# Order of VectorE's level loop and a second value block in split parts, in the gated-linear-attention mixer of a two-block network

## The reference, cut to what matters

```python
z = x @ w_in                                   # q, k (512 wide each), v (1024), r (1024), gate ranks
loga = log_sigmoid(glr @ gate_w + gate_b) / GLA_TAU
# per direction: decay between positions t >= s is exp(b[t] - b[s]), b = cumsum(loga)
A = einsum('bhtd,bhtsd,bhsd->bhts', q, dec, k) ; o = A @ v (+ carried state)
o = head_norm(o_fwd + o_bwd, norm_g)
h = (silu(r) * o) @ w_out
x = layer_norm(ALPHA * x + h) ; x = layer_norm(ALPHA * x + ec_moe(x))   # 16 experts, 201 MB of weights
```

## Time and profile before

| | |
|---|---|
| median of 3 runs | 1665.46 us (1664.6 to 1666.51) |
| the profiled execution, its own time | 1665.1 us |
| its span, first to last instruction | 1663.3 us |
| mean granted clock of TensorE | 0.902 of full speed |
| TensorE busy | 1324.9 us, 80% of the span |
| VectorE busy | 661.9 us, 40% |
| ScalarE busy | 451.0 us, 27% |
| DMA | 537.91 MB, 323 GB/s over the span |

### The profile page before, as it was taken

The page is one execution under the profiler, slowest core; times in us unless marked ns, Lnnn a source line. Parts: engine busy times, 40 slices in busy tenths (PEclk is TensorE's granted clock), DMA queues, the critical chain, the costliest instruction groups (busy, mean ns, idle before and its releaser), DMA issues.

```text
span 1663.3 us, 20942 instructions
## 1 busy us (share of the span) xinstructions
PE 1324.9 (80%) x8622; PEld 849.0 (51%) x8622; DVE 661.9 (40%) x1083; ACT 451.0 (27%) x736; POOL 23.4 (1%) x47
## 2 busy tenths in 40 slices
PE   9999665375476899994755646559999999999997
PEld 8786121121121486841211212117888889888886
DVE  5664000000010288620000000005877678887767
ACT  4452000000010266510100000003444455654443
POOL 2000000000000100000000000000000000000000
PEclk9999887697696999997976968889999999999999
DMA  9778999999999974899999999999755763075650
GB/s 363 213 297 335 432 430 429 430 431 428 431 431 428 400 280 158 320 384 430 430 430 430 430 430 430 430 427 393 236 177 202 250 205 127 1 254 176 202 202 25
DMA packets 131432, 537.91 MB, mean 323 GB/s; under 512 B 8244, under 2 KB 71988, under 8 KB 104092
## 3 DMA queue, kind: packets, MB, share of 16 engines
q1 hardware_dynamic: 127056, 530.08, 79.8%
q10 hardware_dynamic: 2380, 2.31, 0.9%
q0 software_dynamic: 1920, 4.43, 0.8%
HBM read 534.17 MB, written 2.62 MB: 323 GB/s over the span
## 4 chain that ended last, share of the span: by engine, by line
PE 52%; DMA 37%; DVE 5%; ACT 2%; SPq 2%; issue 1%; DVEq 0%; ACTq 0%
PE bank L952 12%; DMA ring<-in_moe_w_down 10%; DMA ring<-in_moe_w_up 10%; PE bank L2373 9%; PE bank L2411 7%; DMA arena<-in_moe_w_down 7%; PE bank L1516 5%; PE bank L2377 5%; PE bank L1563 5%; DMA moe_slots<-in_moe_w_up 3%; DMA moe_slots<-in_moe_w_down 3%; DMA gk_w<-in_moe_w_up 2%; DMA xT_pair<-in_moe_w_up 2%; PE bank L590 1%; PE bank L1572 1%
## 5 line engine op out<-in xcount | busy, mean ns | idle before, releaser
L1516 PE MATMUL bank<-ring,arena 128*32 128x512 f32 x960 | 216.5, 719 | 74.7 <-DMA arena<-in_moe_w_up 35.6
L868 DVE TENSOR_TENSOR w_lo<-ring,w_hi 128x1024 fp32r<-128x1024 f32 x151 | 183.1, 1222 | 87.3 <-ACT w_hi L863 86.7
L1563 PE MATMUL bank<-ring,arena 128*32 128x512 f32 x496 | 145.9, 718 | 55.7 <-DMA moe_slots<-in_moe_w_down 23.0
L863 ACT ACTIVATE w_hi<-ring 128x1024 fp32r<-128x1024 f32 x151 | 158.7, 1057 | 83.0 <-PE bank L952 37.8
L2373 PE MATMUL bank<-xT_parts,w_hi 128*128 128x512 f32 x496 | 177.1, 399 | 0.0
L1683 DVE TENSOR_TENSOR arena<-arena,bank 64x512 f32<-64x512 f32 x32 | 22.1, 691 | 385.8 <-ACT arena L1623 385.8
L1516 PE MATMUL bank<-moe_slots,arena 128*32 128x512 f32 x352 | 107.6, 766 | 55.0 <-DMA ring<-in_moe_w_up 32.4
L2377 PE MATMUL bank<-xT_parts,w_lo 128*128 128x256 f32 x496 | 139.0, 280 | 0.0
L1516 PEld LDWEIGHTS bank<-ring,arena 128*32 128x32 f32 x960 | 48.7, 128 | 152.0 <-issue 140.4
L1623 ACT ACTIVATE arena<-bank 64x512 f32<-64x512 f32 x32 | 18.9, 589 | 395.8 <-PE bank L1516 395.8
L1516 PE MATMUL bank<-arena 128*32 128x512 f32 x488 | 105.6, 712 | 24.3 <-DMA ring<-in_moe_w_up 14.6
(11 more groups left out here) (381 smaller groups left out, 2481.1 us busy)
## 6 DMA issues: line engine op xcount, KB each, us to landing
ring<-in_moe_w_up SPq DMA_DIRECT2D x24, 2048.0 KB, 39.0
ring<-in_moe_w_down SPq DMA_DIRECT2D x22, 2048.0 KB, 41.5
ring<-in_moe_w_gate SPq DMA_DIRECT2D x20, 2048.0 KB, 39.4
moe_slots<-in_moe_w_gate SPq DMA_DIRECT2D x18, 2048.0 KB, 37.1
arena<-in_moe_w_up SPq DMA_DIRECT2D x14, 2048.0 KB, 37.2
arena<-in_moe_w_gate SPq DMA_DIRECT2D x12, 2048.0 KB, 39.8
ring<-in_w_gate SPq DMA_DIRECT2D x22, 1024.0 KB, 5.1
ring<-in_w_up SPq DMA_DIRECT2D x22, 1024.0 KB, 5.1
```

The lines of the kernel that those rows point to most:

```text
L863: nc.scalar.activation(dst, raw, ACT.Copy).then_inc(hi_ready, 1)
L868: nc.vector.tensor_tensor(lo, raw, hi.bitcast(F32), ALU.subtract).then_inc(split_ready, 1)
L1516: last = nc.tensor.matmul(ps[B_GU[j % 2]][32 * c:32 * c + 32, :], xin[:, j, k, :], w, start=(k == 0), stop=(k == KD - 1), tile_position=(0 ...
L1563: last = nc.tensor.matmul(ps[B_DN[c]][32 * j:32 * j + 32, :], hT[:, j // 2, at:at + CAP], slot_row(ud[j], f % 2)[:, c * HALF:(c + 1) * HAL ...
```

## The change

Three things change. In VectorE's loop, `args(n+2)` moves ahead of `key_query(n+1)`, and some low parts move ahead of `merge(n)`. The value block 1 is split as a whole, like block 0: its first half is no longer plain, so there are two more chunks (30 for 28), two more `hi` and two more `lo`, and TensorE's `project(2)` and `project(3)` become two chunks each. Chunks from 12 on have new numbers: 12 to 15 are block 1, 16 and 17 the split half of block 2, 18 to 21 block 3 and 22 to 29 the output projection. The three buffers are dealt out anew, and ScalarE's list is changed to suit.

```diff
-        MIX_CHUNKS, GLA_CHUNKS, FFN_CHUNKS = 32, 28, 3 * NF
+        MIX_CHUNKS, GLA_CHUNKS, FFN_CHUNKS = 32, 30, 3 * NF
...
-                    sp.wait_ge(chunk_done, (ml_mix.done(29), gla_mix.done(25))[m])
+                    sp.wait_ge(chunk_done, (ml_mix.done(29), gla_mix.done(27))[m])
...
-        gla_mix = Mixer(gla_u[0:6] + gla_u[7:10:2] + gla_u[10:16], 2, chunk0["gla"],
-                        {c: -c % 3 for c in range(10, GLA_CHUNKS)})
-        HALF_FIRST = (8, 12, 14, 16)
-        WHOLE_SPLIT = (0, 3)
+        gla_mix = Mixer(gla_u[0:8] + gla_u[9:16], 2, chunk0["gla"],
+                        {c: (GLA_CHUNKS - 1 - c) % 3 for c in range(11, GLA_CHUNKS)})
+        HALF_FIRST = (8, 12, 16, 18)
+        WHOLE_SPLIT = (0, 1, 3)
...
-                elif n in (2, 4):
-                    value_rows(n // 2 - 1)
-                    hi(act, 12 + n)
+                elif n == 2:
+                    value_rows(0)
+                    hi(act, 14)
                 elif n == 3:
-                    hi(act, 15)
+                    hi(act, 15, 16)
+                elif n == 4:
+                    hi(act, 17)
+                    value_rows(1)
                 elif n == 5:
-                    hi(act, 17, 18)
+                    hi(act, 18, 19)
                 elif n == 6:
                     near_blocks()
                     block_merge(5)
-                    hi(act, 19)
+                    hi(act, 20, 21)
...
             for n in range(len(LEVELS)):
+                if n + 2 < len(LEVELS):
+                    args(n + 2)
                 if n + 1 < len(LEVELS):
                     key_query(n + 1)
+                lo(dve, *{2: (15,), 3: (17,), 5: (19,), 6: (21,)}.get(n, ()))
                 if n < BLOCK_LEVEL:
                     merge(n)
-                if n + 2 < len(LEVELS):
-                    args(n + 2)
-                if n < 6:
-                    lo(dve, *((12, 13), (14,), (15,), (16,), (17, 18), (19,))[n])
-            lo(dve, 20, 21)
+                lo(dve, *{0: (12, 13), 1: (14,), 2: (16,), 4: (18,), 5: (20,)}.get(n, ()))
+            lo(dve, 22, 23)
```

More of the change, by code:

```diff
@@ L969, in token_chunk @@
                 self.products(pe, c, [(ps[banks[i]][:, :], slice(k2 * HALF, (k2 + 1) * HALF),
-                                       (slice(None), c % 4 * 2 + k2, slice(i * P, (i + 1) * P)),
-                                       not onto and c % 4 * 2 + k2 == 0, c % 4 * 2 + k2 == KD - 1, False)
+                                       (slice(None), (c - self.count) % 4 * 2 + k2, slice(i * P, (i + 1) * P)),
+                                       not onto and (c - self.count) % 4 * 2 + k2 == 0, (c - self.count) % 4 * 2 + k2 == KD - 1,
+                                       False)
                                       for i in tiles for k2 in range(2)], operand, more=tiles == (0,))
@@ L2072, in gla_scalar @@
                     value_rows(3)
-                    hi(act, 20, 21)
+                    hi(act, 22, 23)
             head_std(act, 1, 0)
@@ L2078, in gla_scalar @@
             head_scale(act, 1, 1)
-            hi(act, 22)
+            hi(act, 24)
             zT_scalar(act, 1, 1, xT3, lambda k: mix_cols[:, 8 + k:9 + k])
-            hi(act, *range(23, 28))
+            hi(act, *range(25, 30))
         def gla_vector(dve, link):
@@ L2181, in gla_vector @@
             zT_vector(dve, 1, 0, xT3)
-            lo(dve, 22)
+            lo(dve, 24)
             zT_vector(dve, 1, 1, xT3)
-            lo(dve, *range(23, 28))
+            lo(dve, *range(25, 30))
         def gla_sync(sp):
```

## The result

The changed kernel takes 1672.97 us (median of 6 runs, 1670.45 to 1674.37) against 1664.73 of the kernel before beside it (6 runs, 1663.33 to 1666.51). The ratio is 1.0049, with a 95% interval of 1.0039 to 1.0058: 8.2 us slower. The profiled execution took 1672.97 (span 1671.2).

What follows compares the result with a forecast made beforehand. VectorE and TensorE, both nearly full in the level stage, set level 7's start, with a full load stream behind. A 6.1 us shift on the profiled 1665.1 gave 1671.2, with the median's 0.4 1671.5; range 1666.5 to 1675.5.

Steps and rivals of the forecast that it cites:

- low parts too late in VectorE's queue: Level stage: `lo(15)` ready only at 636.28, so TensorE stands for 2.8 us before chunk 15, and again before chunk 19.
- VectorE's waits for levels: Level stage: `args` at the queue's head waits for TensorE's levels, 2.3, 2.0 and 1.1 us, replacing waits for exponentials.
- The timetable: Level stage worked forward: level 1 at 622.1, level 3 639.2, level 4 647.1, level 6 663.6, level 7 667.4 us.
- about 9 us in six places, less its 1.3 saved: TensorE in the level stage: total waits for low parts, against 1.3 us less work without the plain half.
- Chunk 19 takes 2.845: TensorE before level 6: the chunk starts once `lo(19)` is ready at 660.71, putting level 6 at 663.56.
- granted clock still 1.00 from 610 to 700: Sign for the profile after: TensorE's clock would stay full over this stretch.
- rival 3: TensorE's clock falls behind 3 us pauses; a half-speed chunk costs 2.8 more: 1674.3, two spells 1677.1 us; chance 0.08.
- main case: Late low parts and level waits start level 7 6.2 us later; 6.1 carries to the end: 1671.5 us; chance 0.70.
- Rival 1: Level stage: low parts come in time, TensorE's floor starts level 7 2.1 us earlier, at 659.2: 1663.4 us; chance 0.05.
- Rival 2: DMA loads: unit 6's slot comes free early, 4.9 of 6.1 us come back: 1666.7, or 1665.5; chance 0.13.
- the two more high parts on ScalarE: ScalarE: about 0.95 us each, hidden in its 15.0 us of idle time before exponentials.
- the wait for slot 10: SP queue's wait, now for chunk 27 of 30, before 25 of 28: same place relative to the end, costing nothing.

Runs made afterwards that it cites:

- e3: Changed kernel with low parts 15, 17, 19 and 21 moved to the head of their rounds, ahead of `args`: 1664.46 us, ratio 1.0000 to the kernel before.
- e1: Changed kernel with `args(n+2)` put back behind `merge(n)`: 1667.64 us, ratio 1.0019 to the kernel before.
- e2: Kernel before with `args(n+2)` ahead of `key_query(n+1)`, nothing else: 1663.32 us, ratio 0.9994 to the kernel before.
- e9: The changed kernel run again, unaltered: 1673.09 us, ratio 1.0045 to the kernel before.
- e6: Changed kernel with low part 19 alone moved to the head of its round, ahead of `args(7)`: 1668.91 us, ratio 1.0027 to the kernel before.
- e4: Changed kernel with ten small unread matmuls in TensorE's pause before chunk 19: 1671.38 us, ratio 1.0043 to the kernel before.
- e8: Changed kernel with ten small unread matmuls in each long TensorE pause, before chunks 15 and 19: 1671.63 us, ratio 1.0044 to the kernel before.
- e5: Kernel of e3 with `key_query(1)` moved into VectorE's wait before `lo(11)`: 1661.85 us, ratio 0.9986 to the kernel before.
- e7: Kernel of e2 with `key_query(1)` moved as in e5: 1663.04 us, ratio 0.9996 to the kernel before.

## Why the prediction was right

**Direction and mechanism: right, and shown.** The prediction named two causes: low parts too late in VectorE's queue, and `args` at its head waiting for levels. The first is shown by e3, which changes only where four low parts stand and takes the whole loss away. The second by e1: 4.3 us of the stage come back, of which about 1.5 would be the clock. The two don't add up, since they act through each other: `args` waiting at the head costs only where a low part that TensorE needs stands behind it. In e3 `args` is ahead of `key_query` as in the changed kernel, and nothing is lost. e2 shows that neither cause acts while the plain half gives cover. VectorE's waits for levels were forecast as 2.3, 2.0 and 1.1 us and are 2.34, 2.09 and 1.04.

**The timetable: right to 0.4 us over 46.** The rest grew by 0.1 to 0.2 with each of the later pauses: chunk 15 takes 2.95 us behind its pause, not 2.845, and the half chunk 17 takes 647.46 - 645.87 = 1.59, not 1.42. The prediction took its price as the mean of two chunks without a pause.

One sum in the prediction doesn't come out as written: "about 9 us in six places, less its 1.3 saved" would be over 7, not 6.2. The rest is the wait of 0.90 us ahead of level 7, shown in e2, which the kernel before has and the changed one hasn't; that is why level 6 was forecast 7.2 later but level 7 only 6.2. The timetable had this right.

**The size: 8.2 for 6.2.** The step that was mis-sized is the one from chunk 19 to level 6, "Chunk 19 takes 2.845". It took 4.38, since the clock fell; the sign "granted clock still 1.00 from 610 to 700" did not hold. So rival 3 came about, on top of the main case and not in its stead. It had been given 0.08, on the ground that the busy share stays near 0.8. The share was 21.12 of 25 us from 635 to 660, and the clock fell all the same. It fell behind one pause in the changed kernel's profile, behind both in e9 and behind the first in e6. Its price of 2.8, for a chunk at half speed throughout, was an upper end: measured were 1.4, 1.6, 1.2 and 2.5. Without it the stage is 53.2 us (e4, e8), 6.7 more than before.

The time itself came closer than the change did, by luck: it was forecast as 1671.5, 1.5 below 1672.97, while the change was 2.1 above the forecast 6.1. The forecast stood on the median of three runs, 1665.46; the kernel before beside the changed one took 1664.73.

**Rival 1 (only work counts)** was wrong for this order and is what e5 shows for another: TensorE's floor gave 659.2 for level 7, and e5's 44.0 behind level 0 would be 658.7 in the kernel before. It is lower by the 0.4 us that level 1 is no longer late.

**Rival 2 (paid back by transfers)** did not happen. The early load went out 8.9 us earlier, and no time came back by it: DMA was idle again in 652 to 655 (share 0.00). The time moved with the stage, within 1.0 us in nine of the ten rows of the table; e9's profile is one execution with both falls, and its own time, 1675.59, is 11.6 above the median of before, for a stage 10.9 longer.

**Costed at nothing:** the two more high parts on ScalarE, the renumbering and the wait for slot 10. In the timeline after, no instruction of VectorE between levels 1 and 7 waits for a high part, and e5 and e7 differ by what TensorE alone saves. In e3 all three are still there, and the loss is gone. Nothing shows a cost, though none was tried by itself.

## What to carry to other kernels

When a slow operation that needs no preparation is replaced by a faster one that needs some, the cover goes with it: work out when its inputs are due before counting what it saves. In a queue of strict order, an instruction that waits for the consumer must not stand ahead of what the consumer waits for; moving four low parts to the head of their rounds was worth 8 us here, and moving `key_query(1)` into an idle stretch another 2. Add queues forward from a trace, with start-to-start times, for every engine at once: shares of busy time could not have shown this.

## What was not expected of the hardware

TensorE's granted clock fell behind pauses of 2.6 to 2.8 us in a stretch where it was otherwise busy, though not in each execution: behind the pause of 2.6 before chunk 15 it stayed at 1.00 in the profiles of the changed kernel and of e4, and was 0.59 and 0.66 in those of e6 and e9. Behind the pauses of up to 1.35 us, five in one stage, it stayed at 1.00 in e1's profile. With ten small matmuls, 2.39 us in all, in each long pause it was 1.00 throughout e8's. These are single executions; what decides between them is not shown. A chunk behind a long pause also takes about 0.1 us more at full clock (2.94 and 2.95 us in e8 for 2.845).
